# A hybrid SSD / DeltaNet / mixture-of-experts step: DeltaNet inverse on four quadrants of TensorE, state scaling on GpSimd, two gate loads in quarters, one silu moved

## The reference

```
# Mamba-2 SSD, 16 heads of 64, chunks of 128, forward and backward; its output is gated:
y = y.reshape(bsz, seqlen, SSD_WIDTH) * jax.nn.silu(z_s.astype(f32))
# Gated DeltaNet, 8 heads of 128, chunks of 64, forward and backward
t_mat = jnp.where(strict, kk * decay * beta[..., None], 0.0) + jnp.eye(c, dtype=f32)
sol = lax.linalg.triangular_solve(t_mat, rhs, left_side=True, lower=True, unit_diagonal=True)
def step(s, inp):
    v_new = u_i - jnp.einsum('bhck,bhkv->bhcv', w_i, s)
    o = jnp.einsum('bhck,bhkv->bhcv', qd_i, s) + jnp.einsum('bhij,bhjv->bhiv', qk_i, v_new)
    s = s * cd_i[..., None, None] + jnp.einsum('bhck,bhcv->bhkv', kd_i, v_new)
# MoE, 32 experts of 1024 x 512, top 1 group, top 2 experts in it
a = jnp.einsum('td,edf->tef', t, lp['w_gate'][sl]); u = jnp.einsum('td,edf->tef', t, lp['w_up'][sl])
act = jax.nn.silu(a) * u * comb[:, sl, None]
out = out + jnp.einsum('tef,efd->td', act, lp['w_down'][sl])
```

## Time and profile before

| | |
|---|---|
| median of 3 runs | 1209.52 us |
| the profiled execution | 1207.35 us, span 1205.6 us |
| mean granted TensorE clock | 0.956 of full |
| TensorE, VectorE, ScalarE, GpSimd busy | 90%, 45%, 27%, 19% |
| HBM traffic | 278 MB read, 235 GB/s over the span |

### The profile page before, as it was taken

The page is one execution under the profiler, slowest core; times in us unless marked ns, Lnnn a source line. Parts: engine busy times, 40 slices in busy tenths (PEclk is TensorE's granted clock), DMA queues, the critical chain, the costliest instruction groups (busy, mean ns, idle before and its releaser), DMA issues.

```text
span 1205.6 us, 21539 instructions
## 1 busy us (share of the span) xinstructions
PE 1084.9 (90%) x8988; PEld 729.3 (60%) x8988; DVE 538.7 (45%) x970; ACT 324.2 (27%) x756; POOL 224.6 (19%) x180
## 2 busy tenths in 40 slices
PE   3799999998698899999899889998898989998895
PEld 1699999997554689999655454443333333343342
DVE  1576776333755366667520144333333333333344
ACT  2332334356553324545200141110000000000002
POOL 0554555342132222222000110000000000000000
PEclk9899999899896999999999988999999999999998
DMA  9642443225024420010403269899999999999993
GB/s 358 236 141 70 140 141 115 83 82 227 18 86 199 176 73 4 4 38 4 158 1 140 82 258 403 364 425 426 425 425 426 426 425 425 425 425 426 425 426 130
DMA packets 52316, 279.06 MB, mean 231 GB/s; under 512 B 6424, under 2 KB 13848, under 8 KB 32784
## 3 DMA queue, kind: packets, MB, share of 16 engines
q1 hardware_dynamic: 48704, 270.09, 55.6%
q0 software_dynamic: 3536, 7.85, 1.8%
HBM read 278.09 MB, written 4.72 MB: 235 GB/s over the span
## 4 chain that ended last, share of the span: by engine, by line
PE 64%; DMA 23%; DVE 6%; ACT 3%; issue 2%; SPq 1%; POOL 1%; DVEq 0%; ACTq 0%
PE ps L679 18%; DMA ring_b<-in_w_up 16%; PE ps L1087 13%; PE ps L920 7%; DMA ring_a<-in_w_gate 5%; PE ps L846 3%; PE ps L1105 2%; PE ps L855 2%; PE ps L858 2%; DMA ring_b<-in_w_ada 2%; PE ps L627 2%; PE ps L749 1%; PE ps L769 1%; PE ps L905 1%; PE ps L896 1%
## 5 line engine op out<-in xcount | busy, mean ns | idle before, releaser
L679 PE MATMUL ps<-h_hi,w_split 128*128 128x392 f32 x784 | 210.5, 350 | 0.1
L1087 PE MATMUL ps<-ring_b,temp 128*64 128x512 f32 x512 | 124.9, 644 | 33.3 <-DMA ring_b<-in_w_up 33.3
L679 PEld LDWEIGHTS ps<-h_hi,w_split 128*128 128x128 f32 x784 | 145.7, 190 | 4.7 <-POOL w_split L536 0.7
L679 PE MATMUL ps<-h_lo,w_split 128*128 128x392 f32 x392 | 134.6, 343 | 0.0
L536 POOL TENSOR_TENSOR w_split<-ring_a,w_split 128x1024 fp32r<-128x1024 f32 x46 | 110.9, 2410 | 109.0 <-ACT w_split L1218 109.0
L1087 PE MATMUL ps<-ring_a,temp 128*64 128x512 f32 x512 | 114.7, 599 | 6.7 <-DMA ring_a<-in_w_gate 5.6
L1105 PE MATMUL ps<-mix,temp 128*64 128x512 f32 x256 | 114.5, 601 | 2.4 <-issue 0.7
L1105 PE MATMUL ps<-kv,temp 128*64 128x512 f32 x256 | 115.0, 603 | 0.0
L1939 DVE SCALAR_TENSOR_TENSOR temp<-temp,silu_c,ps 128x512 f32<-128x512 f32 x16 | 12.0, 747 | 228.7 <-PE ps L1087 226.7
L1087 PEld LDWEIGHTS ps<-ring_b,temp 128*64 128x64 f32 x512 | 44.1, 147 | 112.4 <-issue 112.4
L1087 PEld LDWEIGHTS ps<-ring_a,temp 128*64 128x64 f32 x512 | 43.2, 138 | 74.9 <-issue 74.6
(11 more groups left out here) (312 smaller groups left out, 1685.8 us busy)
## 6 DMA issues: line engine op xcount, KB each, us to landing
ring_a<-in_w_gate SPq DMA_DIRECT2D x32, 2048.0 KB, 17.3
ring_b<-in_w_up SPq DMA_DIRECT2D x32, 2048.0 KB, 18.0
mix<-in_w_down SPq DMA_DIRECT2D x32, 1024.0 KB, 16.4
kv<-in_w_down SPq DMA_DIRECT2D x32, 1024.0 KB, 18.5
ring_a<-in_w_in SPq DMA_DIRECT2D x11, 2048.0 KB, 7.7
ring_a<-in_w_ada SPq DMA_DIRECT2D x6, 2048.0 KB, 10.1
ring_b<-in_w_ada SPq DMA_DIRECT2D x6, 2048.0 KB, 18.9
ring_a<-in_w_out SPq DMA_DIRECT2D x2, 2048.0 KB, 14.2
```

What stands on the lines that cost most here:

```text
L679: last = nc.tensor.matmul(ps[:, 2 + n % 3, 0:ROW], w[:, k, :], h[:, k, :], start=(k == 0 and x == 0), stop=(k == KD - 1 and x == 2))
L1087: last = nc.tensor.matmul(ps[64 * e:64 * e + 64, 2 + n, :], xg_t[:, k, 64 * e:64 * e + 64], slots[2 * n + e][:, k, :], start=(k == 0), sto ...
```

## The change

Seven edits. (1) Half of the inverse's products go to the quadrants (0, 64) and (64, 0) of TensorE, with a second PSUM bank (banks 6a and 6a + 1 for half a); `HOME`, `STAY` and `MOVE` say which head stands where. (2) VectorE now makes P' = I - off D out of PSUM (128x256), and ScalarE copies D P' and its transpose (128x512), so the subtraction changes place and the two engines change roles. (3) `decay_state` moves from ScalarE (16 activations) to GpSimd (4 tensor operations of 128x512), with its own semaphore. (4) The recurrence's pieces stand at other places between the levels, and `state_products_dn` uses banks 4 and 5 for both halves. (5) `silu(z)` moves behind unit 1 of SSD. (6) The gate weights of pairs 1 and 2 are loaded in quarters, each as soon as the pair before has used that quarter. (7) Some semaphores are merged (`tok_mm` and `cum_mm` into `gate_sums_mm`, `any_ready` into `gd_ready`).

The diff, cut to its core:

```diff
-        BANK_X, BANK_Q, BANK_O = 2, 4, 6
+        HOME = {0: (0, 1, 2, 3), 1: (0, 3, 2, 1)}
+        STAY, MOVE = (0, 2), (1, 3)
+        dn_p_flat = [p.rearrange("p h i -> p (h i)") for p in dn_p]
+
+        def at_home(lev):
+            return HOME[(lev + 1) % 2][0:2], HOME[(lev + 1) % 2][2:4]
+
+        def block_of(lev, h, transposed):
+            if lev == 0:
+                return 4 * transposed + h
+            if lev == 5:
+                return 4 + h
+            if transposed:
+                return 2 + STAY.index(h) if h in STAY else 6 + MOVE.index(h)
+            near, far = at_home(lev)
+            return near.index(h) if h in near else 4 + far.index(h)
+
+        def other(rows):
+            return slice(64 - rows.start, 128 - rows.start)
+
+        def both_banks(a, n):
+            return ps[:, 6 * a:6 * a + 2, 0:n]
...
-            with sp.Fori(1, NPAIR) as i:
+            def pair_loads(i):
                 for s in range(4):
+                    if isinstance(i, int) and s < 2:
+                        continue
                     sp.wait_ge((gate_mm, up_mm)[s // 2], i)
...
+            def gate_quarters(i):
+                for q in range(4):
+                    if q < 3:
+                        sp.wait_ge(gate_part, 3 * i - 2 + q)
+                    else:
+                        sp.wait_ge(gate_mm, i)
+                    for e in range(2):
+                        sp.dma_start(slots[e][:, 2 * q:2 * q + 2, :], w_gate[2 * i + e, :, :].rearrange("(p k) n -> p k n", p=P)[:, 2 * q:2 * q + 2, :]).then_inc(slot_in[e], 16)
+
+            for i in range(1, EARLY + 1):
+                gate_quarters(i)
+                pair_loads(i)
+            with sp.Fori(EARLY + 1, NPAIR) as i:
+                pair_loads(i)
...
+            def decay_state(j, a):
+                pool.wait_ge(ksqs_mm[a], 2 * j)
+                for half, (rows, d, t, _) in enumerate(halves(j)):
+                    st = dn_s[:, DN_STEPS[j][0], d, 512 * a:512 * a + 512].rearrange("p (h v) -> p h v", h=4)
+                    cd = 48 + rows.start // 4 + 8 * d + 4 * a
+                    last = nc.gpsimd.tensor_tensor(st, st, g_tot[:, t, cd:cd + 4].unsqueeze(2).to_broadcast([P, 4, P]), ALU.mult)
+                last.then_inc(st_decayed[a], 1)
+
             for j in range(NJ):
                 for n in (1, 3, 5, 7, 9):
                     inverse_step(j, n)
+                    if j >= 2 and n in (1, 5):
+                        decay_state(j - 1, n // 4)
...
-                        for h in range(4):
-                            for rows, at in quads:
-                                last = nc.tensor.matmul(A[rows, h, :], off[rows, h, :], mask("eye")[rows, :] if lev == 0 else d[rows, h, :],
-                                                        start=True, stop=True, tile_position=at)
...
+                            for i, (h_near, h_far) in enumerate(zip(*at_home(lev))):
+                                for rows, at in quads:
+                                    nc.tensor.matmul(near[rows, i, :], off[rows, h_near, :], dd[rows, block_of(lev - 1, h_near, 0), :],
+                                                     start=True, stop=True, tile_position=at)
+                                for rows, at in quads:
+                                    last = nc.tensor.matmul(far[other(rows), i, :], off[rows, h_far, :], dd[rows, block_of(lev - 1, h_far, 0), :],
+                                                            start=True, stop=True, tile_position=(rows.start, 64 - rows.start))
                         last.then_inc(lev_mm1[a], 1)
...
                         if lev < 5:
-                            for h in range(4):
+                            for i in range(2):
+                                hn, hf = h_near[i], h_far[i]
                                 for rows, at in quads:
-                                    nc.tensor.matmul(A[rows, h, :], dt[rows, h, :], prod[rows, h, :], start=True, stop=True, tile_position=at)
-                        for h in range(4):
+                                    nc.tensor.matmul(near[rows, i, :], dd[rows, block_of(lev - 1, hn, 1), :], prod[rows, product_of(hn), :],
+                                                     start=True, stop=True, tile_position=at)
+                                for rows, at in quads:
+                                    nc.tensor.matmul(far[other(rows), i, :], dd[rows, block_of(lev - 1, hf, 1), :], prod[rows, product_of(hf), :],
+                                                     start=True, stop=True, tile_position=(rows.start, 64 - rows.start))
+                        for i in range(2):
+                            hn, hf, c = (STAY[i], MOVE[i], 2 + i) if lev < 5 else (h_near[i], h_far[i], i)
                             for rows, at in quads:
-                                last = nc.tensor.matmul(B[rows, h, :], prod[rows, h, :], dt[rows, h, :], start=True, stop=True, tile_position=at)
+                                nc.tensor.matmul(near[rows, c, :], prod[rows, product_of(hn), :], dd[rows, block_of(lev - 1, hn, 1), :],
+                                                 start=True, stop=True, tile_position=at)
+                            for rows, at in quads:
+                                last = nc.tensor.matmul(far[other(rows), c, :], prod[rows, product_of(hf), :], dd[rows, block_of(lev - 1, hf, 1), :],
+                                                        start=True, stop=True, tile_position=(rows.start, 64 - rows.start))
                         last.then_inc(lev_mm2[a], 1)
...
                     pe.wait_ge(vn_ready[a], j + 1)
-                    if j:
-                        pe.wait_ge(sr_scaled[a], 2 * j - 1)
+                    if a:
+                        pe.wait_ge(s_ready[0], j + 1)
+                    elif j:
+                        for half in range(2):
+                            pe.wait_ge(sr_scaled[half], j)
...
-                state_products_dn(j, (1,))
+                inner_products(j, (0,))
                 inverse_step(j + 1, 7)
                 inverse_step(j + 1, 8)
-                inner_products(j, (0,))
+                state_products_dn(j, (1,))
...
+                more = 0 if n else 48 * (min(i, EARLY) if isinstance(i, int) else EARLY)
                 for e in range(2):
-                    pe.wait_ge(slot_in[2 * n + e], i * 16 + 16 * (n_loads[2 * n + e] + 1))
+                    pe.wait_ge(slot_in[2 * n + e], i * 16 + 16 * (n_loads[2 * n + e] + 1) + more)
                 for k in range(KD):
+                    if k in (2, 4, 6) and n == 0 and isinstance(i, int) and i < EARLY:
+                        last.then_inc(gate_part, 1)
...
-            act.wait_ge(block_out, NB - CONV_BLOCKS)
-            nc.scalar.activation(mix[:, :, :], mix[:, :, :], ACT.Silu).then_inc(z_ready, 1)
-            nc.scalar.preload_act_table_set("natural_log_exp_and_others")
...
+                if n == 1:
+                    act.wait_ge(block_out, NB - CONV_BLOCKS)
+                    nc.scalar.activation(mix[:, :, :], mix[:, :, :], ACT.Silu).then_inc(z_ready, 1)
+                    nc.scalar.preload_act_table_set("natural_log_exp_and_others")
...
             def level(j, n):
+                lev = (n - 2) // 2
                 for a in range(2):
-                    act.wait_ge(lev_mm1[a], 6 * j + (n - 1) // 2 + 1)
-                    nc.scalar.copy(dn_p[a], ps[:, a, 0:256].rearrange("p (h i) -> p h i", h=4)).then_inc(lev_p[a], 1)
+                    act.wait_ge(lev_mm2[a], 5 * j + lev)
+                    at = 0 if lev < 5 else 256
+                    nc.scalar.copy(dn_dd[a][j % 2][:, at:512].rearrange("p (b i) -> p b i", b=2), both_banks(a, 256 - at // 2)).then_inc(d_ready[a], 1)
...
-            def decay_state(j, a):
-                seq = DN_STEPS[j][0]
-                for rows, d, t, _ in halves(j):
-                    for h in range(4):
-                        st = dn_s[:, seq, d, (4 * a + h) * P:(4 * a + h + 1) * P]
-                        cd = 48 + rows.start // 4 + 8 * d + 4 * a + h
-                        last = nc.scalar.activation(st, st, ACT.Identity, scale=g_tot[:, t, cd:cd + 1])
-                last.then_inc(sr_scaled[a], 1)
...
-                level(j + 1, 3)
-                if j:
-                    decay_state(j, 0)
-                level(j + 1, 5)
+                level(j + 1, 4)
                 scaled_values(j)
-                level(j + 1, 7)
-                if j:
-                    decay_state(j, 1)
-                level(j + 1, 9)
+                level(j + 1, 6)
+                level(j + 1, 8)
+                level(j + 1, 10)
                 if j == 3:
                     square_outputs(0)
-                level(j + 1, 11)
...
-                        V.tensor_tensor(dn_dt[a][g], eye4, dn_off[a][0], ALU.subtract)
+                        V.tensor_tensor(dn_dt[a][g][:, 0:2, :], eye4[:, 0:2, :], dn_off[a][0][:, 0:2, :], ALU.subtract)
```

(18 more changed lines are left out.)

92 lines of the change are left out of this document (56 added, 36 removed).

## The result

The changed kernel takes 1190.14 us (median of 4 runs, 1188.75 to 1192.45), the kernel before 1208.28 in the same comparison: ratio 0.9855, 95% interval 0.9825 to 0.9884. The forecast was 1184. The profiled execution took 1190.96 us, its span is 1189.2, against 1207.35 and 1205.6.

What follows compares the result with a forecast made beforehand. TensorE was taken to bound DeltaNet, full DMA the experts' weights; 1207.35 - 21 (DeltaNet) - 0 (silu) - 3.2 (quarters) = 1183 us for the profiled execution, forecast 1184, range 1168 to 1212.

Steps and rivals of the forecast that it cites:

- Quadrants at 14.5 ns: TensorE's 64x64 products in DeltaNet's inverse: four quadrants at once start an instruction each 14.5 ns instead of 29.
- 25 ns floor: Rival, chance 0.14: TensorE's start-to-start time never drops below about 25 ns; DeltaNet -3 us, total 1201.
- quadrants don't overlap: Rival, chance 0.16: TensorE stays at 29 ns and the new order costs; DeltaNet +8 us, 1216 against the median.
- First step -4.5: DeltaNet's first step, without reads and remainders: 27.6 to 22.7 us, taken as -4.5.
- Steps at 26.3: Each of the four DeltaNet steps after the first goes from 29.4 to 26.3 us.
- the new wait behind `end_values`: Level 1 of a step: TensorE's second product waits for VectorE's P', queued behind `end_values`; 13.4 us instead of 11.9.
- Four steps alike, -12.4: The four DeltaNet steps after the first each go from 29.4 to 26.3 us, together -12.4.
- First inverse -4: DeltaNet's first inverse, with no recurrence to fill TensorE: five levels at 0.8 us less each, -4.
- DeltaNet -21: Whole DeltaNet part: four steps -12.4, first step -4.5 and first inverse -4, in all -21 us.
- Silu 0: SSD: moving the silu only moves TensorE's gap from 301-306 to 308-313 us; gain 0, bounds -3 and +2.
- Quarters -3.2: Experts' gate loads: early quarters close a 4.2 us DMA gap, a 1.0 gap comes; net -3.2, bounds -4.2 and 0.
- State scaling hidden on GpSimd: DeltaNet steps: four GpSimd operations of about 1.4 us each on a mostly idle engine; contention on VectorE 0.3 a step.

Runs made afterwards that it cites:

- end_late: Kernel after, with VectorE making P' of level 1 before the end values in each of the five steps; 1186.45 us, ratio 0.9831.
- sums_late: Kernel after, with VectorE's sums of the output squares behind its last level's subtraction in the step with j = 3; 1184.75 us, ratio 0.9827.
- hold_out: Kernel after, with the 2 MB load of output weights held from the first inverse to the end of step 1's inverse; 1185.68 us, ratio 0.9827.
- at_once: Kernel after, with the gate quarters of pairs 1 and 2 all issued when the last pair's gate products are done; 1192.36 us, ratio 0.9880.
- combo2: Kernel after with the edits of `hold_out`, `sums_late` and `end_late`, and VectorE's eight SSD normalisations spread over steps 0 to 3; 1180.74 us, ratio 0.9776.
- silu_alone: Kernel before with one edit: the silu and its table loads stand behind unit 1's exponentials; 1205.61 us, ratio 0.9982.

## Why the prediction was right, point by point

- *Quadrants at 14.5 ns*: right, and with it the rivals "25 ns floor" and "quadrants don't overlap" are out. The 25 ns that the Trainium skill gives as the least start-to-start time ("TensorE: Matmul & The Clock Gate", section "Wait — 56ns, not 53.3ns?") does not hold across four tiles: the trace has 14.3 ns from one instruction to the next.
- *First step -4.5*: -4.48 from n = 1 to n = 1. By the prediction's own marks, a step's first instruction (L818, L870), it is 27.57 to 25.24, so -2.3: the half clock behind the gap fell on the first 5 us of that step, which my table counts to the first inverse. *Steps at 26.3*: 26.88 and 26.34; the new wait behind `end_values` was there, 0.97 us, worth 1 us a step by `end_late`.
- *Four steps alike, -12.4* is where the step with j = 3 failed. Before, TensorE's 2.8 us a level covered a sum that stood ahead of the last subtraction; now it is on the path: +0.4 instead of -3.1, 3.1 of it undone by `sums_late`.
- *First inverse -4*: +1.4. I followed the engines and left out the supply of instructions, though before's chain had 0.69 us of it at 429.51. `hold_out` shows 26.73 against before's 30.04, so -3.3 was there, and the load beside it took 4.8 (gap 2.8 and the half clock behind it).
- *DeltaNet -21*: -10.6 to the last turn. The missing 10.4 are 5.4 of the first inverse and 3.5 of j = 3, the rest mostly 0.6 in step 1 and 0.7 in step 4.
- *Silu 0*: -6.25, outside my bounds (-3 to +2). The queue of ScalarE went as I wrote (the copy ahead of unit 2 starts at 312.25, before 312.45), but I took everything behind the gap to be as slow as before. Not looked at: L1665's 2.50 us for what else takes 0.42, though the earlier trace rows showed the mechanism. It accounts for 2 to 3.5 of the 6.
- *Quarters -3.2*: -3.6 by `at_once` against after. It doesn't show between before and after, since TensorE ran L1127, L1158 and pair 1's gate and up products in 4.96, 1.83 and 16.37 us instead of 3.78, 1.04 and 15.44 (half clock, 726 to 736), 2.9 us in the stretch that sets pair 2's load.
- *State scaling hidden on GpSimd*: right; an operation takes 1.02, not 1.4. Back on ScalarE it costs 5 us of DeltaNet.

So the mechanism of the quadrants was right at its size, and that 1190 came out near 1184 is partly luck: 10 us too much for DeltaNet, 5 too much for the experts (+1.6 for -3.2), and against them 6 too little for SSD and 1 for what stands between. The sum has a slip of 1 us too: 1183 for the profiled execution is 1185 for the median.

## What to carry to other kernels

When one engine stops being the bound, every order on the other engines that it used to cover has to be read again, step by step and not by the typical step: here two orders on VectorE were worth 3 us once and 1 us a step. Look for rows that take several times what their siblings take, and at what stands beside them on GpSimd; here one such row was worth 2 us or more. Large loads should not land beside a dense stream of small matmuls: "issue" in the chain, of 0.69 us already in the kernel before, is the sign, and a stream that starts twice as often makes more of it.

## What the hardware showed that I had not expected

- TensorE started instructions of 64x64 matmuls every 14.3 ns on four tiles, but they don't always arrive as fast: beside 2 MB of loads it stood still for 2.7 to 3.9 us in the eight executions with such a stream and a load beside it, one of them with the load elsewhere, and 1.23 us once with idle DMA engines. It went on 1.2 to 1.6 us behind the end of a 16 KB packet of the instruction queue, every time.
- A VectorE operation with two inputs in SBUF hardly advances while a GpSimd operation runs: 0.42 us became 2.50 with 2.21 of overlap, and 0.68 became 1.23 with 0.68 (L1827, beside L611). One with an input in PSUM, L1711 at 324.93 in after, kept its 1.28 beside GpSimd's L595.
- Idle gaps of TensorE of 2 to 5 us were followed by stretches at 1.2 GHz (granted clock 0.50 in 424 to 428, 0.66 in 532 to 534 of after, 0.53 in 312 to 318). In `combo2` 1.23 us was enough (0.57 in 422 to 426); 1.80 in SSD was not (1.00 behind it in `silu_alone`).
- Eight DMAs of 0.5 MB issued together moved 351 and 412 GB/s in the two windows shown. Issued as their places came free they moved 296 and 368, with the DMA engines' share at 1.00 and 0.99; why the rate is lower there is open.
